# A hybrid diffusion step on one core: h's parts added on VectorE, the mLSTM norm inside the first seven gate units, attention's parts split sooner, the gate row turned later

## What is computed

```
h = rmsnorm(x, g_pre_mix) * (1 + scale1) + shift1
(na_q, na_k, na_v, m_q, m_k, m_v, m_o, m_i, m_f, cv_b, cv_c, cv_x, gate_pre) = split(h @ w_in)
hm = hm * rsqrt(mean(hm * hm, -1) + EPS)
hm = merge_heads(hm) * m_norm_g * sigmoid(m_o)
g  = sigmoid(gate_pre + b_gate).reshape(B, N, 3, D_MODEL)
merged = g[0] * (att @ w_br_na) + g[1] * (hm @ w_br_m) + g[2] * (hc @ w_br_cv)
x = x + gate1 * rmsnorm(merged @ w_out, g_post_mix)
ff = (silu(h2 @ w_ffn_gate) * (h2 @ w_ffn_up)) @ w_ffn_down
x = x + gate2 * rmsnorm(ff, g_post_ffn)
```

## Time and profile before

| | us |
|---|---|
| median of 3 runs | 1145.93 (1145.84 to 1146.75) |
| the profiled execution, its own time | 1146.42 |
| its span, first to last instruction | 1144.6 |
| PE busy | 1111.0 (97%) |
| DVE busy | 797.5 (70%) |
| ACT busy | 511.5 (45%) |
| POOL busy | 106.1 (9%) |
| granted TensorE clock, mean | 0.992 |

### The profile page before, as it was taken

One profiled execution on the slowest core, in us unless ns is written; L12 is line 12 of the kernel. 1 busy time (PEld: TensorE's weight loads), 2 busy tenths in 40 slices (PEclk: granted clock), 3 DMA queues, 4 the chain that ended last, 5 costly groups with the idle time before them and its releaser, 6 DMA issues.

```text
span 1144.6 us, 18655 instructions
## 1 busy us (share of the span) xinstructions
PE 1111.0 (97%) x7228; PEld 1048.2 (92%) x7228; DVE 797.5 (70%) x1401; ACT 511.5 (45%) x958; POOL 106.1 (9%) x153
## 2 busy tenths in 40 slices
PE   6999999999999999899979999999999999999997
PEld 4799899899999999899969988999999999988886
DVE  5748888768575656888758736899897777633444
ACT  5534444445333433355533237645555555533431
POOL 2051332000000002401100002000000000000002
PEclk9999999999999999999989999999999999999999
DMA  9676554342521112035365434244422232315112
GB/s 362 233 235 199 163 150 150 111 147 80 73 71 56 56 60 71 2 117 180 122 210 177 150 113 150 72 143 134 130 97 88 75 128 94 111 60 196 57 37 92
DMA packets 42919, 141.79 MB, mean 124 GB/s; under 512 B 9392, under 2 KB 10960, under 8 KB 41168
## 3 DMA queue, kind: packets, MB, share of 16 engines
q1 hardware_dynamic: 38752, 131.64, 35.4%
q0 software_dynamic: 4080, 8.97, 2.4%
HBM read 127.93 MB, written 12.60 MB: 123 GB/s over the span
## 4 chain that ended last, share of the span: by engine, by line
PE 83%; DVE 9%; ACT 2%; issue 2%; DMA 2%; SPq 0%; POOL 0%; POOLq 0%; DVEq 0%; ACTq 0%
PE ps L2368 26%; PE ps L2369 25%; PE ps L2370 25%; DMA ada<-in_w_first 1%; DVE w_lo L1686 1%; PE ps L2626 1%; PE ps L2641 1%; PE ps L2688 1%; DMA raw<-in_w_blocks 1%; ACT w_hi L1241 1%; PE ps L2690 1%; PE ps L2600 1%; PE ps L2692 1%; DVE tq L1999 1%; DVE prod_a L1700 1%
## 5 line engine op out<-in xcount | busy, mean ns | idle before, releaser
L2370 PE MATMUL ps<-h_hi,w_lo 128*128 128x320 f32 x1024 | 316.8, 309 | 0.0
L2369 PE MATMUL ps<-h_lo,w_hi 128*128 128x320 f32 x864 | 267.6, 310 | 0.0
L2368 PE MATMUL ps<-h_hi,w_hi 128*128 128x320 f32 x800 | 252.7, 316 | 5.4 <-ACT mo L1334 5.2
L2370 PEld LDWEIGHTS ps<-h_hi,w_lo 128*128 128x128 f32 x1024 | 192.6, 188 | 0.0
L2369 PEld LDWEIGHTS ps<-h_lo,w_hi 128*128 128x128 f32 x864 | 162.9, 189 | 0.1
L2368 PEld LDWEIGHTS ps<-h_hi,w_hi 128*128 128x128 f32 x800 | 150.8, 189 | 7.4 <-issue 6.7
L2368 PE MATMUL ps<-w_hi,h_hi 128*128 128x512 f32 x378 | 148.6, 393 | 0.0
L1686 DVE TENSOR_TENSOR w_lo<-raw,w_hi 128x1024 fp32r<-128x1024 f32 x93 | 116.3, 1261 | 45.3 <-ACT w_hi L1241 44.0
L2370 PE MATMUL ps<-w_hi,h_lo 128*128 128x512 f32 x378 | 147.2, 389 | 0.0
L2369 PE MATMUL ps<-w_lo,h_hi 128*128 128x512 f32 x378 | 147.2, 389 | 0.0
L1241 ACT ACTIVATE w_hi<-raw 128x1024 fp32r<-128x1024 f32 x93 | 96.8, 1052 | 74.4 <-PE ps L2370 70.0
(11 more groups left out here) (312 smaller groups left out, 2058.4 us busy)
## 6 DMA issues: line engine op xcount, KB each, us to landing
raw<-in_w_blocks SPq DMA_DIRECT2D x182, 512.0 KB, 3.9
ada<-in_w_first SPq DMA_DIRECT2D x8, 1024.0 KB, 20.2
gdram<-stage SPq DMA_DIRECT2D x8, 640.0 KB, 6.7
gt<-gdram SPq DMA_DIRECT2D x8, 640.0 KB, 4.9
xline<-x SPq DMA_DIRECT2D x5, 512.0 KB, 5.0
x<-xline SPq DMA_DIRECT2D x5, 512.0 KB, 8.2
xt<-in_x_sample SPq DMA_DIRECT2D x4, 512.0 KB, 6.0
condr<-in_cond_rows POOLq DMA_DIRECT2D x2, 1024.0 KB, 8.9
```

Source lines behind the costliest of these rows:

```text
L2368: nc.tensor.matmul(dst, wh, xh, start=first, stop=False, skip_group_check=resumed)
L2369: nc.tensor.matmul(dst, wh, xl, start=False, stop=False, skip_group_check=resumed)
L2370: return nc.tensor.matmul(dst, wl, xh, start=False, stop=last, skip_group_check=resumed)
```

## The change

`reb` moves from GpSimd to DVE and becomes four steps `reb 0..3`, the first two behind mo group 0, the third behind group 2, the fourth behind group 4. `gsum 3` and the `gsplit` steps move: `gsplit 0` from group 3 to 4, `gsplit 1` from 4 to 5, `gsplit 2` and `gsum 3` to group 6 (from 5 and 4). The `hm` steps are put down by a table over units 0 to 6, all five blocks, none in unit 7 and none among the branch units. In unit 7 `att_split` 0 and 1 stand at q = 3 and 4 (from 3 and 5), the splits of B0+1 at q = 5 and of B0+2 and B0+3 at q = 6 (from 3, 5 and 6). The turn of the gate row, its store and its spreading move to branch units 2 and 4.

```diff
-        behind = {0: [("ada_turn", 2), ("ada_store", 2)],
+        behind = {0: [("reb", 0), ("reb", 1)],
                   1: [("wsum", 0), ("wop", 0, 0), ("wop", 0, 1)],
-                  2: [("gsum", 0)],
-                  3: [("gsum", 1), ("gsum", 2), ("gsplit", 0), ("wop", 0, 2), ("wop", 0, 3)],
-                  4: [("gsplit", 1), ("gsum", 3)],
-                  5: [("gsplit", 2), ("wop", 0, 4), ("wop", 0, 5)],
+                  2: [("gsum", 0), ("reb", 2)],
+                  3: [("gsum", 1), ("gsum", 2), ("wop", 0, 2), ("wop", 0, 3)],
+                  4: [("gsplit", 0), ("reb", 3)],
+                  5: [("gsplit", 1), ("wop", 0, 4), ("wop", 0, 5)],
+                  6: [("gsum", 3), ("gsplit", 2)],
                   7: [("gsplit", 3)]}
-        plan.append(("reb",))
+        norm = {0: [(4, 0, 0)], 1: [(2, 1, 0), (3, 0, 1), (4, 2, 0)], 2: [(2, 1, 1), (4, 2, 1)], 3: [(3, 0, 2)],
+                4: [(2, 1, 2), (3, 0, 3), (4, 2, 2)], 5: [(2, 1, 3), (3, 0, 4), (4, 2, 3)], 6: [(2, 1, 4), (4, 2, 4)]}
...
                 plan.append(("wu", w, q))
-                if q == 2:
-                    plan.append(("hm", w % 2, c))
-                if q == 4 and w % 2:
-                    plan.append(("hm", 2, c))
-                if w >= 2 and q == 2:
-                    plan.append(("gload", w - 2)) if w == 2 else None
+                plan.extend(("hm", sub, c) for at, sub, c in norm.get(w, []) if at == q)
+                if (w, q) == (2, 2):
+                    plan.append(("gload", 0))
                 if w == NG - 1:
-                    if q in (1, 3, 5, 6):
-                        split_to(d0 + (1, 3, 5, 6).index(q) + 1)
-                    if q in (3, 5):
-                        plan.append(("att_split", q // 2 - 1))
+                    if q in (3, 4):
+                        plan.append(("att_split", q - 3))
+                    if q in (1, 5):
+                        split_to(d0 + (1 if q == 1 else 2))
+                    if q == 6:
+                        split_to(d0 + 4)
...
-                if u == 0 and j < 2:
-                    plan.extend([("hm", 0, 4)] if j == 0 else [("hm", 1, 4), ("hm", 2, 4)])
                 if (u, j) == (1, 0):
                     plan.append(("hm_split",))
-                if (u, j) == (1, 2):
-                    plan.append(("ada_rows", 2))
+                if (u, j) in ((2, 0), (2, 2), (4, 0)):
+                    plan.append(("ada_turn" if j == 0 and u == 2 else "ada_store" if u == 2 else "ada_rows", 2))
...
-                elif step[0] == "reb":
-
-                    pool.wait_ge(ml_h, len(ML_UNITS))
-                    pool.wait_ge(merged_add, 16)
-                    for dst, k0, h in ((tq12, 0, 1), (tq22, 4, 1), (tq11, 0, 0), (tq21, 4, 0)):
-                        nc.gpsimd.tensor_tensor(dst[:, :, :], h_hi[:, k0:k0 + 4, half(h)].bitcast(F32),
-                                                h_lo[:, k0:k0 + 4, half(h)].bitcast(F32),
-                                                ALU.add).then_inc(reb_done, 1)
...
+                elif step[0] == "reb":
+                    j = step[1]
+                    if j == 0:
+                        dve.wait_ge(ml_h, len(ML_UNITS))
+                        dve.wait_ge(merged_add, 16)
+                    k0, h = ((0, 1), (4, 1), (0, 0), (4, 0))[j]
+                    nc.vector.tensor_tensor((tq12, tq22, tq11, tq21)[j][:, :, :], h_hi[:, k0:k0 + 4, half(h)].bitcast(F32),
+                                            h_lo[:, k0:k0 + 4, half(h)].bitcast(F32), ALU.add).then_inc(reb_done, 1)
...
                     if c:
                         pe.wait_ge(hm_out, c)
-                        pe.wait_ge(gl_row, 1)
...
                     if q == 0:
-                        pe.wait_ge(ml_h, len(ML_UNITS))
+                        pe.wait_ge(hm_out, TT)
```

More of the change, by code:

```diff
@@ L286, in gate_stretch @@
         for w in range(NG):
-            c = w // 2
             for q in range(7):
                 plan.append(("wu", w, q))
-                if q == 2:
-                    plan.append(("hm", w % 2, c))
-                if q == 4 and w % 2:
-                    plan.append(("hm", 2, c))
-                if w >= 2 and q == 2:
-                    plan.append(("gload", w - 2)) if w == 2 else None
-                if w == NG - 1:
-                    if q in (1, 3, 5, 6):
-                        split_to(d0 + (1, 3, 5, 6).index(q) + 1)
-                    if q in (3, 5):
-                        plan.append(("att_split", q // 2 - 1))
+                plan.extend(("hm", sub, c) for at, sub, c in norm.get(w, []) if at == q)
+                if (w, q) == (2, 2):
+                    plan.append(("gload", 0))
+                if w == NG - 1:
+                    if q in (3, 4):
[4 more added lines that the diff above has]
+                        split_to(d0 + 4)
         plan.append(("gates_end",))
```

## The result

| | before | changed |
|---|---|---|
| median, same chip, 4 runs each | 1146.28 us | 1133.14 us (1132.46 to 1133.89) |
| ratio, 95% interval | | 0.9887 (0.9871 to 0.9903) |
| the profiled execution | 1146.42 | 1132.46 |
| its span | 1144.6 | 1130.7 |

A forecast was written before the change was run, and what follows sets the result against it. The prediction took TensorE, busy 97% of the span, as the bound; 7.2 + 10.1 = 17.3 us off the profiled 1146.42 gave 1129.1, and 1128.6 for the median, range 1126.6 to 1133.5 (its own case 1126.8 to 1130.5).

The forecast's parts named there:

- Part 1: Mo groups to gate unit 0: additions on DVE cut PE's wait from 5.4 to 0.8 us; 7.2 us gained.
- The loss beside a GpSimd instruction: Mo groups: each GpSimd mo instruction that meets a DVE instruction costs DVE 0.24 us.
- Part 2: Norm inside units 0 to 6: no PE wait for scaling, slack 1.2 us in unit 1, 0.5 in unit 5.
- rival C: Units 1, 2, 4, 5, 6: DVE scales each block too late, five stalls of 7.5 us, 1166; chance 0.02.
- Unit 6's turn: Gate unit 6: the turn moved there from the branch stretch costs at most 0.60 us, taken as 0.5.
- Part 3: Unit 7 and branch units 0 and 1: the stretch from branch unit 0 to 2 gains 10.65 us, 10.1 less unit 6's turn.
- its two losses: Branch units 1 and 2: PE waits for late DVE drains, 0.3 us and 0.75 us lost.
- the landing of branch unit 1's gates: Gate load issued about E + 7.7, landing 4.9 us later at the median, 7.6 at most, which costs 0.7 more.
- E: The start of branch unit 0, from which the forecast counts its times.
- rival B: Branch start: DVE's backlog or the gate load holds units 1 and 2 for 3 us more, 1131.6; chance 0.12.
- Part 4: Gate row's turn, copy and store in branch unit 2, spreading in unit 4: zero cost.
- A: Mo tail stays late: 2.5 us lost, 1131.1, or 1133.7 with a clock drop; chance 0.1.

The follow-up runs named there:

- reb_pool: The changed kernel with the four additions of h's parts back on GpSimd, in the new order of steps; 1138.55 us.
- reb_dve_old_order: The changed kernel with all four additions on DVE behind mo group 0, gsum and gsplit in the old order; 1131.91 us.
- gl_early: The changed kernel with the load of branch unit 1's gates issued at the end of gate unit 7, ahead of the weight loads and store; 1129.97 us.
- hm_later: The changed kernel with the split of the mLSTM's parts at branch unit 2 in place of 1; 1133.52 us.
- hm_old: The changed kernel with the mLSTM norm at its old places, block 4 behind branch group 0; 1139.92 us.
- r_after: The changed kernel run again with no edit, as the level for its batch; 1132.01 us.
- att_old: The changed kernel with unit 7's steps at their old places, attention's second split at q = 5; 1131.90 us.
- ada_old: The changed kernel with the turn, stores and spreading of the gate row at their old places; 1133.23 us.
- best: The changed kernel with early gate load, the mLSTM's split at branch unit 2 and B0+3's split between branch unit 0's drains; 1128.70 us.
- best_again: The kernel of best run again without edit, as the level for the next batch; 1129.29 us.
- best2: The kernel of best, with gate unit 0's first product waiting only for the mo group that last used its own bank; 1127.92 us.

## Why the prediction was right, and what it missed

**Part 1 held to 0.1 us**, 7.1 against 7.2. DVE's timeline in the changed kernel:

```profile
450.99 1.23 DVE L1676 TENSOR_TENSOR w_lo<-raw,w_hi 128x1024 fp32r<-128x1024 f32 x1 [0.31 <-ACT w_hi L1231]
452.13 2.89 DVE L1988 TENSOR_TENSOR tq<-h_hi,h_lo 128x1280 f32<-128x1280 f32 x2
...
475.20 1.74 DVE L1997 TENSOR_TENSOR tq<-tq,tq 128x1280 f32<-128x1280 f32 x1
```

The weight split is back from 3.90 to 1.23; two additions take 2.89, so 1.41 to 1.48 each, the lower end of what was bounded by 3.4. gsum 3 ended 27.3 us after the first mo matmul (475.20 + 1.74 - 449.63); the forecast had 27.4 (475.8 less the 448.38 at which the mo groups began before). The loss beside a GpSimd instruction was 1.74 - 1.48 = 0.26 where GpSimd met it, against 0.24. The wait was 0.8 and the clock stood. What the forecast ascribed to the parts together, reb_pool and reb_dve_old_order share out: with the additions on DVE, all of it to the engine, none to the order.

**Part 2 held.** In unit 1 the scaling of block 0 ended and its turn began 1.2 us apart, and in unit 6, the last, 1.7 us; in unit 5, for which the forecast had 0.5, it was 1.8, so no lateness was carried over:

```profile
497.97 0.69 DVE L2265 TENSOR_TENSOR hsum<-hsum,small 128x512 f32<-128x512 f32 x1
...
560.87 0.69 DVE L2265 TENSOR_TENSOR hsum<-hsum,small 128x512 f32<-128x512 f32 x1
```
```profile
499.91 0.60 PE L2698 MATMUL ps<-cst,hsum 128*128 128x128 f32 x4
...
563.25 0.60 PE L2698 MATMUL ps<-cst,hsum 128*128 128x128 f32 x4
```

No turn waited, so rival C had no ground. Unit 6's turn costs what was put down for it, 0.48 of 0.5.

**Part 3 missed by one term.** The mechanism and the DVE queue were right, as gl_early shows, with 15.11 for 15.15. That the sum fits so closely is luck in part: its two losses were 0.50 and 0.53 us from start to start, where 0.3 and 0.75 were forecast. The mis-sized term is the landing of branch unit 1's gates: issued at E + 7.8 as computed, it was taken at the 4.9 us of the median, and the 7.6 of the longest load was kept for the range; it took 8.6 and 8.2 us in the two traces of this kernel, and 9.3 in hm_later. The median of a transfer's landing times was the wrong row, since this load goes out while two weight loads (1 MB) and a 640 KB store are still under way; the window of 0.92 DMA share around the wait says the same:

```profile
594.20:596.60 2.40, 0.26 (x3) 0.00 (x0) 0.49 (x1) 1.21 (x2) 0.00 (x0) 1.00 0.92 355
```

The row of this very load in the kernel before was there to be read, and would not have been enough either; 6.8 us would have had it landed at E + 14.5, just in time:

```profile
gt<-gdram SPq DMA_DIRECT2D x1, 640.0 KB, 6.8
```

There one weight load and the store were under way when it was issued; here it was two and the store. What came is the forecast's rival B by its mechanism, with 1.95 us where B said 3.

**Part 4 held**: nothing to be measured either way.

**The sum.** 17.3 less 1.95 (gates) less 0.1 (the rest) is 15.2, which is the traces' 690.0 - 674.8. Another 1.2 went in the part before the mo groups, which has the same instructions in both kernels. The forecast took that part as fixed. Over the traces of this study its end lies between 447.78 (hm_old) and 451.09 (reb_pool), 3.3 us apart, and the two traces of the changed kernel differ by 1.4. This is the spread of one kernel's runs, and it came out against the forecast. PE's first waits for x, at the very start, are 9.6 us in the changed kernel against 8.8 in the one before, 0.8 of the 1.2 (the longest of them is 7.8 to 8.9 us over the traces); why they spread is open. The spread also took the median 0.5 below the profiled execution; for the changed kernel it was 0.7 above. So of the 4.5 us between 1128.6 and 1133.1, 2.1 are terms of the sum, 1.2 the part before the mo groups and 1.2 the place of the median; more than half is spread, and it took the result out of the forecast's own 1126.8 to 1130.5 into the part of the range that was there for A and B.

The 0.7 may be the clock. The profiled execution of the changed kernel has a mean clock of 0.999, the other three 0.998, 0.997 and 0.997, and by estimate 0.001 of the clock over 1131 us is 1.1 us. In the six kernels with a wait of 1.8 to 3.0 us in the branch units (changed, r_after, hm_later, att_old, ada_old, reb_dve_old_order) 10 of 24 executions stand at 0.997; in gl_early, best, best_again and best2, without that wait, none of 17 is under 0.998. That fits a fall of the clock behind this wait in some executions, on top of the wait itself. Of these six only att_old's trace shows such a fall, so it is not shown for the changed kernel.

## What to carry to other kernels

An engine that is idle is not free: GpSimd's additions cost DVE more (10.7 us) than DVE needed for them (5.95 for the four in a row in reb_dve_old_order), so before work is put on GpSimd, look at what DVE's two-input instructions beside it cost. When a stall is taken out, follow every queue to the next wait, DMA issue queues too, and price a transfer by the company in which it then goes out, not by its median; here moving one load ahead of three others was worth 2 us. Price a stall of PE with the half clock that may follow it: in three traces it came behind a wait of 2.0 to 2.6 us. Compare traces from a common mark behind the noisy part, since stretches repeated to 0.02 us where medians moved by 1.

## What the runs showed of the hardware

GpSimd's own instruction stretches too. In the changed kernel the scaling of one mo tile took from 0.46 us, where DVE stood idle, to 1.61 beside it (minimum, median, maximum in ns), while DVE lost 0.24 to 0.26 a time:

```profile
L1180 POOL TENSOR_SCALAR mo<-mo x8: 460/1102/1606, 453.9 to 478.6; 128x320 f32<-128x320 f32 x8
```
The Trainium skill (SBUF — State Buffer, Who interferes with whom) has the loser blocked for the whole of the other's instruction; GpSimd's 1.61 less 0.46 is 1.15, under the 1.41 of DVE's 128x1280 instruction, and agrees with it, as does DVE's 3.46 less 0.69, or 2.77, beside a GpSimd addition that takes 2.97 undisturbed (reb_pool); but DVE's 0.24 is half of GpSimd's undisturbed 0.46, so here the measurement decides.

The length of a gap alone doesn't tell whether the clock falls. Gaps of 2.2 (changed), 2.7 (ada_old), 2.8 (hm_later) and 3.0 us (reb_dve_old_order) left it at 1.00; a gap of 2.0 in att_old was followed by 0.66, one of 2.3 in reb_pool by 0.63, and one of 2.6 in the kernel before by 0.50. Behind gaps of 4.0, 5.2 and 8.7 us, the only longer ones of these stretches that began at full clock, it fell each time. The first window is reb_pool's, the other two those of the kernel before:

```profile
603.70:607.00 3.30, 3.29 (x15) 3.29 (x16) 3.19 (x8) 0.00 (x0) 0.00 (x0) 0.63 0.09 37
```
```profile
588.50:590.00 1.50, 1.41 (x6) 0.89 (x6) 1.11 (x2) 0.35 (x1) 0.00 (x0) 1.00 0.84 205
590.00:595.90 5.90, 0.01 (x1) 0.01 (x1) 4.18 (x6) 1.57 (x3) 1.81 (x3) 0.50 0.45 131
```

The last two set a reading of the forecast right. It took the clock to have stayed at 1.00 across the gap of 2.6 us, from a window that ends with the gap, at 588.50, and put the half clock behind it down to the wait of 5.9. But that wait began at 589.98, and the clock was down by 590.04, 0.06 us later, so the fall belongs to what came before it: 2.6 us idle and 1.45 us of matmuls. A wait of over 2 us was thus not safe in the forecast's own trace. That the wait of 2.2 us at branch unit 2 was not followed by a fall in the profiled execution of the changed kernel is luck.
